# The gated recurrence of a two-block network, computed by blocks of 128 tokens instead of over all pairs of tokens

## The reference

```python
z = h @ w_in                                   # 1024 -> 3104 columns: q, k (after a conv and silu), v, o, gates
b = jnp.cumsum(fj, axis=-1)                    # fj: log of the forget gate
D = jnp.where(lower, b[..., :, None] - b[..., None, :] + ij[..., None, :], -jnp.inf)
m_t = jnp.maximum(b + m[..., None], jnp.max(D, axis=-1))
s = jnp.einsum('bhtd,bhsd->bhts', qj, kj) * jnp.exp(D - m_t[..., None])
num = jnp.einsum('bhts,bhsv->bhtv', s, vj) + w_inter[..., None] * jnp.einsum('bhvd,bhtd->bhtv', C, qj)
den = jnp.sum(s, axis=-1) + w_inter * jnp.einsum('bhd,bhtd->bht', n, qj)
h = num / jnp.maximum(jnp.abs(den), jnp.exp(-m_t))[..., None]
```

## Time and profile before

| What | Value |
|---|---|
| Time, median of 3 runs | 2607.58 us (2604.2 to 2609.79) |
| Profiled execution | 2616.13 us, span 2614.3 us |
| PE busy in the span | 2507.3 us (96%) |
| DVE, ACT, POOL busy | 1252.2 us, 917.9 us, 45.4 us |
| Mean granted clock of PE | 0.973 of full speed |

### The profile page before, as it was taken

One profiled execution on the slowest core, in us unless ns is written; L12 is line 12 of the kernel. 1 busy time (PEld: TensorE's weight loads), 2 busy tenths in 40 slices (PEclk: granted clock), 3 DMA queues, 4 the chain that ended last, 5 costly groups with the idle time before them and its releaser, 6 DMA issues.

```text
span 2614.3 us, 30378 instructions
## 1 busy us (share of the span) xinstructions
PE 2507.3 (96%) x12260; PEld 2061.1 (79%) x12260; DVE 1252.2 (48%) x1548; ACT 917.9 (35%) x1257; POOL 45.4 (2%) x64
## 2 busy tenths in 40 slices
PE   7989999999999899999999999999988999999998
PEld 6658888888986678888878888799866977788886
DVE  6678533366627553332354442446585523544423
ACT  3453333213345333331233331334444434433311
POOL 0200000000000000000000000000000000000000
PEclk9998999998999899999999999999988999999999
DMA  8125522472220022222222222221100330222221
GB/s 337 56 114 195 192 95 96 167 279 84 81 97 1 17 81 96 96 96 97 97 81 96 96 98 95 90 100 65 65 17 17 129 113 33 81 96 96 97 97 64
DMA packets 37029, 261.44 MB, mean 100 GB/s; under 512 B 4112, under 2 KB 4368, under 8 KB 5840
## 3 DMA queue, kind: packets, MB, share of 16 engines
q1 hardware_dynamic: 31248, 219.87, 23.4%
q0 software_dynamic: 5696, 40.37, 4.0%
HBM read 258.13 MB, written 2.10 MB: 100 GB/s over the span
## 4 chain that ended last, share of the span: by engine, by line
PE 86%; DVE 8%; ACT 4%; issue 1%; DMA 1%; SPq 0%; DVEq 0%; ACTq 0%
PE bank L222 24%; PE bank L224 24%; PE bank L223 24%; PE bank L1737 2%; DVE w_lo L209 1%; ACT w_hi L205 1%; PE bank L325 1%; DMA work<-stream 1%; PE bank L2017 1%; PE bank L1712 1%; PE bank L2100 1%; PE bank L253 1%; PE bank L254 1%; PE bank L259 1%; PE bank L2112 1%
## 5 line engine op out<-in xcount | busy, mean ns | idle before, releaser
L222 PE MATMUL bank<-h_hi,w_hi 128*128 128x512 f32 x1880 | 741.1, 394 | 6.8 <-DVE h_lo L564 2.3
L224 PE MATMUL bank<-h_hi,w_lo 128*128 128x512 f32 x1880 | 735.4, 391 | 0.0
L223 PE MATMUL bank<-h_lo,w_hi 128*128 128x512 f32 x1880 | 735.0, 391 | 0.0
L209 DVE TENSOR_TENSOR w_lo<-raw,w_hi 128x2048 fp32r<-128x2048 f32 x192 | 440.0, 2292 | 589.1 <-ACT w_hi L205 589.1
L205 ACT ACTIVATE w_hi<-raw 128x2048 fp32r<-128x2048 f32 x192 | 366.3, 1908 | 425.9 <-PE bank L224 417.1
L222 PEld LDWEIGHTS bank<-h_hi,w_hi 128*128 128x128 f32 x1880 | 355.2, 189 | 86.5 <-issue 8.4
L224 PEld LDWEIGHTS bank<-h_hi,w_lo 128*128 128x128 f32 x1880 | 355.0, 189 | 75.0
L223 PEld LDWEIGHTS bank<-h_lo,w_hi 128*128 128x128 f32 x1880 | 355.3, 189 | 73.5 <-issue 0.5
L222 PE MATMUL bank<-g_hi,w_hi 128*128 (+1 forms) x704 | 279.1, 396 | 0.0
L223 PE MATMUL bank<-g_lo,w_hi 128*128 (+1 forms) x704 | 279.1, 396 | 0.0
L224 PE MATMUL bank<-g_hi,w_lo 128*128 (+1 forms) x704 | 279.1, 396 | 0.0
(11 more groups left out here) (278 smaller groups left out, 2763.7 us busy)
## 6 DMA issues: line engine op xcount, KB each, us to landing
raw<-stream SPq DMA_DIRECT2D x192, 1024.0 KB, 4.8
work<-stream POOLq DMA_DIRECT2D x19, 1024.0 KB, 6.6
h_plain<-stream POOLq DMA_DIRECT2D x16, 1024.0 KB, 5.5
work<-stream SPq DMA_DIRECT2D x13, 1024.0 KB, 12.5
x<-xT SPq DMA_DIRECT2D x1, 2048.0 KB, 9.5
outT<-work SPq DMA_DIRECT2D x8, 256.0 KB, 2.2
work<-even_tables POOLq DMA_DIRECT2D x1, 1024.0 KB, 9.4
work<-memT POOLq DMA_DIRECT2D x1, 1024.0 KB, 5.1
```

What stands on the lines that cost most here:

```text
L209: nc.vector.tensor_tensor(w_lo[:, slot(m), :], raw[:, slot(m), :], w_hi[:, slot(m), :], ALU.subtract).then_inc(lo_split, 1)
L222: nc.tensor.matmul(out, stationary[0], moving[0], start=first, stop=False)
L223: nc.tensor.matmul(out, stationary[0], moving[1], start=False, stop=False)
L224: return nc.tensor.matmul(out, stationary[1], moving[0], start=False, stop=last)
```

## The change

The weights are now formed only in the four diagonal blocks of 128 x 128. What lies before (or, backwards, after) a block comes through a state: for each direction, and for each of the three borders between blocks, a matrix of keys by values for all tokens on the far side.

- During the units: `factors`, `scale_keys` (DVE) and 16 transposes bring the keys into token order and scale them, six pieces for each direction. `add_state` (PE) forms the states, 48 matmuls of 129 columns after unit 9 and 48 after unit 10, each with an output of 64 partitions, in turns the lower and the upper half (head 2p and head 2p + 1). `copy_state` (ACT) takes them out of PSUM.
- The rows `m`, and the rows `reach` (the maximum at the border minus `m`, exponentiated on ACT), go to device memory by a DMA, and come back spread over the partitions by DMAs that ACT issues (`load_reach`: 128 x 2 x 512 for a head, `load_queries`: two of 64 x 2 x 384 for a pair of heads). `spread` is gone.
- The mask is added by GpSimd (`gpsimd`), 16 instructions of 128 x 512.
- In the loop, ACT takes four exponentials of 128 x 128 per q instead of seven pieces of 1280 columns. `weigh` is one instruction of 512 columns instead of four of 1280 in all. The scores are 8 matmuls of 128 columns for a pair of heads, in turns on the lower and upper 64 rows of the array.
- `sum_values` has 7 matmuls of 129 columns instead of 10: four with 128 rows (diagonal block times values, `near`) and three with 64 rows (scaled queries times state, `far`), alternating. The two directions have banks of their own, so a sum waits for the division two steps back.
- `divide` has three small instructions instead of four; forwards the scaling is one instruction instead of four. `scale_queries` (DVE, two instructions for a pair of heads) is new.

```diff
             def scalar(self, act, st):
                 for u in range(13):
+                    if u == 12:
+                        self.exps(act, st, 0)
+                        self.exps(act, st, 1)
+                        act.wait_ge(self.s_moved, 48)
+                        self.load_queries(act, 1)
                     act.wait_ge(unit_used, m + 1)
...
+                    if u in (10, 11):
+                        for i in range(4):
+                            self.copy_state(act, 4 * (u - 10) + i)
+                    if u == 11:
+                        self.load_queries(act, 0)
-                for q in range(2 * self.H):
+                for q in range(2, 2 * self.H):
...
+            def gpsimd(self, pool):
+                for q in range(2 * self.H):
+                    h, d = q // 2, q % 2
+                    if d == 0:
+                        pool.wait_ge(self.s_landed[h % 2], 16 * (h // 2 + 1))
...
+                    nc.gpsimd.tensor_tensor(md, md, hide, ALU.add).then_inc(self.s_masked, 1)
...
+            def add_state(self, pe, d, p):
+                i = 4 * d + p
+                if i >= 4:
+                    pe.wait_ge(self.s_copied, i - 3)
+                for n, (j, a) in enumerate(self.PIECES[d]):
+                    for k in range(2):
+                        h = 2 * p + k
+                        last = nc.tensor.matmul(bank[64 * k:64 * k + 64, 4 + i % 4, j * self.N:(j + 1) * self.N],
+                                                self.keys[d][:, n, h * 64:h * 64 + 64], self.v[:, a, h, :],
...
             def sum_values(self, pe, q):
-                if q:
-                    pe.wait_ge(self.s_out, q)
+                if q >= 2:
+                    pe.wait_ge(self.s_out, q - 1)
...
+                    far = 0 <= j < self.REFS
+                    if far:
+                        nc.tensor.matmul(outs[t], self.qs[p % 2][half, d, j * P:j * P + P],
+                                         self.c[4 * d + p][half, j, :], start=True, stop=False)
+                    last = nc.tensor.matmul(outs[t], self.se[:, q % 2, t * P:t * P + P], self.v[:, t, h, :],
+                                            start=not far, stop=True)
```

More of the change, by code:

```diff
@@ new lines, in tensor @@
+                        nc.tensor.matmul(bank[:, 6, 320:368], ones[0:R, :],
+                                         self.picks[0:R, :, :].rearrange("p j c -> p (j c)"), start=True,
+                                         stop=True).then_inc(self.s_pe_prep, 1)
+                    if u == 7:
+                        pe.wait_ge(self.s_silu, 8)
+                        pe.wait_ge(self.s_dve_prep, 3)
+                        for a in range(TB):
+                            for p in range(4):
+                                last = nc.tensor.transpose(bank[:, 4 + a, p * P:p * P + P],
+                                                           self.qk[:, 4 + p, a * P:a * P + P], ident)
+                            last.then_inc(self.s_pe_prep, 1)
@@ new lines, in score @@
+            def score(self, pe, p):
+                if p == 0:
+                    pe.wait_ge(self.s_evac, 12)
+                elif p == 1:
+                    pe.wait_ge(self.s_evac, 13)
+                else:
+                    pe.wait_ge(self.s_se, 4 * p - 4)
+                for a in range(TB):
+                    t = slice(a * P, a * P + P)
+                    for k in range(2):
+                        half = slice(64 * k, 64 * k + 64)
+                        last = nc.tensor.matmul(bank[:, (2 + 2 * p + k) % 4, t], self.qk[half, 4 + p, t],
+                                                self.qk[half, p, t], start=True, stop=True)
+                last.then_inc(self.s_scored, 1)
@@ L1732, in sum_values @@
                 for t in range(TB):
-                    blocks = range(0, t + 1) if d == 0 else range(t, TB)
-                    out = bank[:, 6 + t // 2, (t % 2) * (P + 1):(t % 2 + 1) * (P + 1)]
-                    for a in blocks:
-                        c = self.SEG[d][a] + t * P - self.span(d, a)[0]
-                        last = nc.tensor.matmul(out, self.se[:, q % 2, c:c + P], self.v[:, a, h, :],
-                                                start=(a == blocks[0]), stop=(a == blocks[-1]))
+                    j = t if d else t - 1
```

298 lines of the change are left out of this document (177 added, 121 removed).

## The result

The changed kernel takes **2624.48 us** (median of 5 runs, 2618.59 to 2625.2), the kernel before 2607.89 on the same chip (median of 5). The recorded ratio is 1.0048, with a 95% interval of 1.0033 to 1.0063: slower, by 0.33 to 0.63%. It is the record's own estimate and not the quotient of these two medians, which is 1.0064; the 19 runs of the kernel before in the next batch have a median of 2611.97. The forecast was 2585.1 us and faster, so it was wrong, and 2624.5 lies outside its range too. A second set of runs, on another occasion, gave 1.004 [1.0026, 1.0055].

What follows compares the result with a forecast made beforehand. PE was taken to bound the units, and nearly the loop, beside a chain through DVE. Saving 46.2 us in the loop and adding 23.7 in the units gave -22.5 us: 2585.1 us, range 2571 to 2604.

Steps and rivals of the forecast that it cites:

- the part on the start: Loop start: PE idles some 5 us, the clock is 0.50 for about 8 us (+4.0 us), then full again.
- rival 2: From unit 10 on the clock stays at 1.2 GHz; net +6.4 us, 2614.0 us, slower; chance 0.10.
- the change of rows: Value sums in the loop: each switch between 64 and 128 rows costs 0.07 us; twelve cost 1.0 with some room.
- Units: Work added to the units ahead of the loop, all on PE's path: together 23.7 us.
- the key products: After unit 9 PE waits for twelve key products on DVE: +1.2 us.
- the copy: After unit 10 the second states wait for a free bank until ACT's first state copy: +3.5 us of idle PE.
- the split of unit 5: Four new DVE instructions stand ahead of the split that unit 5 already waits for: +1.4 us.
- Rival 1: The state matmuls in the units do not overlap; price 9.8 us, 2594.9 us; chance 0.13.
- Start: Loop start: DVE's last split, two query products and 0.5 us for late ACT put the first weighing 6.7 us after unit 12.
- Beat of 5.8: Loop: PE, DVE, ACT and the chain all close together, giving 5.8 us per head (5.3 to 6.5).
- Locks between DVE and GpSimd: Loop: DVE and GpSimd lock each other out of SBUF; at the worst 17 us more, leaving a gain of 5.
- Rival 3: Loop: the broadcasts of reach rows land late, a beat of 9.7 us; net +4.7 us, 2612.3 us; chance 0.05.

Runs made afterwards that it cites:

- e3_far128: Changed kernel with far sums on all 128 rows, adding the states of both heads of a pair (result not the reference's): 2588.76 us, ratio 0.9914.
- e2_filler: Changed kernel plus eight unread matmuls of 512 columns filling PE's wait between the first scores and the first value sum: 2607.72 us, ratio 0.9976.
- e4_near64: Changed kernel with near sums on 64 rows, leaving out half of a block's tokens (result not the reference's): 2593.87 us, ratio 0.9934.
- e8_four_changes: Changed kernel with the same sums reordered, so four changes of rows per sum instead of six: 2602.23 us, ratio 0.9967.
- e10_mask_dve: As e7_again, but DVE adds the masks instead of GpSimd: 2587.07 us, ratio 0.9914.
- e7_again: Changed kernel with zero-masked queries and 128-row far sums, states copied one unit earlier, eight filling matmuls after the first scores; repeat run: 2586.15 us.

## Why the prediction was wrong

**The step that failed** is in the part on the start: "After that, PE at 80 to 90% of its time: in `Even` a window with PE busy 3.70 of 5 us had the full clock, so I let it stand." It did not: the windows of the loop have 0.50, with PE busy 4.00 of 4. The row chosen as evidence shows a busy share, and the busy share did not tell: e3_far128 has the full clock at 5.26 of 8. That window of `Even` was no likeness of the new loop either: of its 35 records only 4 are on 64 rows, and these take turns between the halves. e3_far128 differs from the changed kernel in the rows of its far sums alone. This was rival 2, "the clock stays at 1.2 GHz", with 0.10; it named 2614.0 and the half array among its reasons. It was too small by 10 us for the second reason:

**A term that was mis-sized: the change of rows.** It was priced at 0.07 us, from one case in the earlier trace rows, where 128 rows are followed by 40. It measures 0.20 at 2.4 GHz and 0.3 at 1.2 GHz, twelve times per head: 2.4 or 3.6 us where the sum had 1.0. Why the one case in the earlier trace rows came out cheaper is not explained; that pair is of another length and width, and no run varied these. A second kind of change in the kernel before, from a pass of 512 columns to the 64 rows of L1396, looks as cheap (93.83 to 94.15, where passes start 0.23 apart: 0.09), so the old trace would not have given the price. With twelve changes PE needs 12 x 0.42 + 2 x 0.22 = 5.5 us per head and the scores 0.5: 6.0 at the full clock. The one beat of e2_filler that lies wholly at the full clock is 6.7; it holds all scores of a pair, for which 5.5 + 1.1 = 6.6. At 1.2 GHz PE needs 12 x 0.72 + 2 x 0.43 = 9.5, and with half of the scores of a pair (2.1, the difference of the beats 9.6 and 11.7) 10.6, where rival 2 had 8.6. The Trainium skill says in TensorEngine Tiling (Array Packing), Key Properties, that changing the mode drains the engine. These traces agree, and the price is above the 0.13 that the prediction gave to a full drain.

**Where the 33.6 us went** (91.9 - 58.3). The first head with the start and the last division took 19.9 us (18.8 until 814.02, and 1.1) for the forecast's 6.7 + 5.8 + 4.0 + 1.2 = 17.7: 2.2. The seven further beats took 886.06 - 814.02 = 72.0, 10.3 each, for 7 x 5.8 = 40.6: **31.4**. Neither error alone explains these. What PE needs per head, estimated from the starts above, with the measured beats beside it:

| | Full clock | 1.2 GHz |
|---|---|---|
| no change of rows in the sums | 14 x 0.22 + 0.5 = 3.6 (e3_far128: beat 5.8) | 14 x 0.43 + 1.1 = 7.1 (e4_near64, at 0.50 to 0.79: beat 6.6) |
| twelve changes | 6.0 (e2_filler: 6.7, with the scores of a pair) | 10.6 (changed kernel: beat 10.3) |

The other engines and the chain through them close a beat of 5.8 anyway. So the changes at the full clock would have cost at most about 7 x 0.9 = 6 us, and the low clock without the changes 7 x 0.8 = 6. Only both together make PE the limit by far, and that is the rest, some 19 us or more. The filled wait of e2_filler (16.8 us in the median) and the fewer changes of e8_four_changes (22.3) each give back a large part of it.

Point by point:

- **Units**: +23.2 for +23.7, but partly by luck. The terms for the key products (1.09 for 1.2) and the copy (3.39 for 3.5) were right, the split of unit 5 took 1.1 for 1.4. State matmuls overlap: 96 records in 5.50 us are 0.057 apart, the forecast had 0.065; both sets at the full clock would be 11.0 for 12.4. Rival 1 is out. The clock cost 7.17 - 5.50 = 1.7 in the second set, for 3.0. Against these stands the low clock behind the wait of unit 5, 3.4 us, which the forecast did not have at all. What is left for the transposes and the small matmul is 1.5, for 2.2.
- **Start**: the first weighing began 7.4 us after unit 12, not 6.7. The timeline of the changed kernel, DVE and then POOL:

```profile
798.61 3.16 DVE L209 TENSOR_TENSOR w_lo<-raw,w_hi 128x2048 fp32r<-128x2048 f32 x1 [9.69 <-ACT w_hi L205]
801.70 1.01 DVE L1718 TENSOR_TENSOR work<-work 128x384 f32<-128x384 f32 x2
802.63 1.28 DVE L1727 SCALAR_TENSOR_TENSOR work<-bank,work 128x512 f32<-128x512 f32 x2
...
797.14 2.49 POOL L1596 TENSOR_TENSOR work<-work,tab 128x512 f32<-128x512 f32 x2 [91.49 <-DMA work<-mlstm_rows]
```

  The split took 3.16 us instead of the 2.29 of the earlier trace rows, beside GpSimd's first two masks, and in e10_mask_dve, without them, 2.29 again. ACT's copy of unit 12 was 0.5 us late behind a table load.
- **Beat of 5.8**: right where no sum changes rows. In e3_far128 it is (846.25 - 805.86) / 7 = 5.8, in e7_again 6.2. The estimates for DVE, ACT and the chain never came to bear in the changed kernel, since PE was slower than all of them. That their sum fits e3_far128 is a mean over beats from 4.9 to 7.7 us, and which of them closes the beat was not separated.
- **Locks between DVE and GpSimd**: the Trainium skill's SBUF — State Buffer, "SBUF: two separate sides", was given a worst case of 17 us. In kind the traces agree: the query products L1718 take 895 ns in the changed kernel, and 614 for the like in e10_mask_dve, where GpSimd is idle. In size it is small, and taking GpSimd out changed nothing that can be measured.
- **Rival 3**, late broadcasts: out. A landing took 4.7 us, and no exponential in the loop waited for a mask.

**What stays open**: which part of the low clock comes from the pauses at the changes, and which from the rows at rest. e4_near64 shows that rows at rest are enough to hold it at 0.50 to 0.79, and e8_four_changes that the clock is higher in most runs with fewer pauses on the same rows. A kernel with pauses but full rows was not tried. Nor is it known why the clock rises for one stretch in one run of the changed kernel and not in the next.

## What to carry to other kernels

Do not alternate matmuls of 64 and of 128 rows: here it cost 0.2 us a time at the full clock, and with the half rows it kept PE at 1.2 GHz. Two errors that each hide below another limit can cost much together: by the estimates above, neither the changes nor the low clock alone would have cost more than some 6 us here. Filling the other half with zeros took two more DVE instructions per pair of heads and turned +0.5% into -0.6%. When you look for what the clock will be, look for a row whose matmuls use the array as the new ones will, not for one whose busy share is alike; a PE that is recorded as busy without a gap can still be at half speed.

## What the runs showed of the hardware that was not expected

- PE busy 8.00 of 8 us and a granted clock of 0.50, for 30 us and more; beside it 5.26 of 8 us and 1.00. The Trainium skill, TensorE: Matmul & The Clock Gate, Part 1, has the clock depend on how busy the PE has been. With "busy" as the profile records it, these rows do not agree.
- A change between 64 and 128 rows: 0.20 us at 2.4 GHz, 0.3 at 1.2 GHz, in both directions.
- The same instructions took 25 us more or less from run to run (e8_four_changes), with the mean clock.
- Matmuls on alternate column halves (L1816) started 0.057 us apart per record, half of the 0.117 of full-width ones in the earlier trace rows, and kept the full clock for 5.5 us.
- Beside two masks of GpSimd DVE's split took 3.16 us, and 2.29 without them (e10_mask_dve).
